# Modulation parts made by VectorE inside the feed-forward stages, with VectorE also making the weights' low halves there

## The reference

```python
def adaln_chunks(cond, w_mod, b_mod):
    m = jax.nn.silu(cond) @ w_mod + b_mod
    return jnp.split(m[:, None, :], N_MOD, axis=-1)          # N_MOD = 9, D = 1024

def pre(h, g, shift, scale):
    return rms_norm(h, g) * (1 + scale) + shift

def swiglu(h, w1, w3, w2):
    return (jax.nn.silu(h @ w1) * (h @ w3)) @ w2             # D_FF = 2816

mx = adaln_chunks(c, w_mod[i], b_mod[i])                      # tokens
mc = adaln_chunks(c_ctx[None], w_mod[i], b_mod[i])            # context
h_x = h_x + 0.5 * mx[2] * ffn1(pre(h_x, g_norm[i, 0], mx[0], mx[1]))
...                                                           # mixer with mx[3..5], ffn2 with mx[6..8]
```

## Time and profile before

| | us |
|---|---|
| median of three runs | 2426.44 (2426.08 to 2431.41) |
| the profiled execution | 2429.39 |
| its span in the trace | 2427.6 |
| PE busy | 2303.7 (95%) |
| DVE busy | 952.8 (39%) |
| ACT busy | 785.6 (32%) |
| POOL busy | 1027.7 (42%) |

### The profile page before, as it was taken

One profiled execution on the slowest core, in us unless ns is written; L12 is line 12 of the kernel. 1 busy time (PEld: TensorE's weight loads), 2 busy tenths in 40 slices (PEclk: granted clock), 3 DMA queues, 4 the chain that ended last, 5 costly groups with the idle time before them and its releaser, 6 DMA issues.

```text
span 2427.6 us, 36791 instructions
## 1 busy us (share of the span) xinstructions
PE 2303.7 (95%) x14268; PEld 1829.4 (75%) x14268; DVE 952.8 (39%) x1611; ACT 785.6 (32%) x1239; POOL 1027.7 (42%) x473
## 2 busy tenths in 40 slices
PE   6998789999879999999999999999999999898999
PEld 2688766767658888887887888887888887547999
DVE  4468646765551131135364121124122114755212
ACT  2443423333323212213223222223222222434443
POOL 0446512323424444443443444443444443304888
PEclk8999879999989999999999999999999999989999
DMA  7334425544543433233432433232433332203655
GB/s 248 91 101 130 148 96 190 178 157 171 216 153 130 130 96 91 90 95 102 150 96 87 165 96 92 91 96 80 164 96 96 96 95 71 76 0 94 184 181 182
DMA packets 82681, 297.37 MB, mean 122 GB/s; under 512 B 9072, under 2 KB 11504, under 8 KB 82288
## 3 DMA queue, kind: packets, MB, share of 16 engines
q1 hardware_dynamic: 82400, 295.03, 37.7%
q10 hardware_dynamic: 144, 0.34, 0.0%
HBM read 294.28 MB, written 1.05 MB: 122 GB/s over the span
## 4 chain that ended last, share of the span: by engine, by line
issue 52%; PE 22%; POOL 19%; DVE 5%; ACT 1%; POOLq 1%; DVEq 0%; ACTq 0%
POOL w_lo L520 19%; PE bank L544 4%; PE bank L548 4%; PE bank L545 4%; PE bank L588 2%; PE bank L1296 1%; PE bank L1307 1%; DVE box L1075 1%; PE bank L919 1%; PE bank L1261 1%; PE bank L1279 0%; PE bank L1252 0%; DVE boxr L1105 0%; DVE boxr L1075 0%; DVE gdn_outer L1646 0%
## 5 line engine op out<-in xcount | busy, mean ns | idle before, releaser
L520 POOL TENSOR_TENSOR w_lo<-w_raw,w_hi 128x1024 fp32r<-128x1024 f32 x383 | 935.4, 2447 | 1175.0 <-ACT w_hi L772 1174.7
L544 PE MATMUL bank<-n_hi,w_lo 128*128 128x512 f32 (+1 forms) x2216 | 799.5, 361 | 31.7 <-POOL w_lo L520 19.5
L548 PE MATMUL bank<-n_lo,w_hi 128*128 128x512 f32 (+1 forms) x2216 | 790.0, 357 | 0.6 <-DVE n_lo L696 0.3
L545 PE MATMUL bank<-n_hi,w_hi 128*128 128x512 f32 (+1 forms) x2216 | 787.3, 355 | 0.0
L772 ACT CAST w_hi<-w_raw 128x1024 fp32r<-128x1024 f32 x383 | 401.2, 1049 | 775.1 <-PE bank L548 768.3
L544 PEld LDWEIGHTS bank<-n_hi,w_lo 128*128 128x128 f32 x2216 | 423.1, 191 | 114.0 <-issue 43.1
L548 PEld LDWEIGHTS bank<-n_lo,w_hi 128*128 128x128 f32 x2216 | 422.7, 191 | 69.0 <-DVE n_lo L696 2.4
L545 PEld LDWEIGHTS bank<-n_hi,w_hi 128*128 128x128 f32 x2216 | 424.8, 192 | 62.6
L2018 DVE TENSOR_TENSOR prod<-silu,bank 128x512 f32<-128x512 f32 (+1 forms) x88 | 54.6, 621 | 727.4 <-PE bank L548 720.1
L544 PE MATMUL bank<-g_hi,w_lo 128*128 128x512 f32 (+1 forms) x768 | 285.2, 371 | 1.1 <-DVE g_lo L2009 1.1
L548 PE MATMUL bank<-g_lo,w_hi 128*128 128x512 f32 (+1 forms) x768 | 283.4, 369 | 0.0
(11 more groups left out here) (315 smaller groups left out, 2017.9 us busy)
## 6 DMA issues: line engine op xcount, KB each, us to landing
w_raw<-in_stream SPq DMA_DIRECT2D x383, 512.0 KB, 3.6
mod_raw<-in_modstream SPq DMA_DIRECT2D x64, 512.0 KB, 5.4
late<-in_modstream SPq DMA_DIRECT2D x56, 512.0 KB, 4.6
w_raw<-in_modstream SPq DMA_DIRECT2D x48, 512.0 KB, 5.2
h<-in_tokens SPq DMA_DIRECT2D x1, 2048.0 KB, 10.2
consts<-in_consts SPq DMA_DIRECT2D x1, 1152.0 KB, 10.0
h<-in_ctx SPq DMA_DIRECT2D x1, 1024.0 KB, 7.5
out<-h SPq DMA_DIRECT2D x8, 128.0 KB, 3.4
```

Source lines behind the costliest of these rows:

```text
L520: nc.gpsimd.tensor_tensor(w_lo[:, slot, :], w_raw[:, slot, :], w_hi[:, slot, :].bitcast(F32), ALU.subtract).then_inc(w_lo_ready, 1)
L544: nc.tensor.matmul(out_ap, wl, hi, start=start, stop=False)
L545: nc.tensor.matmul(out_ap, wh, hi, start=False, stop=False)
L548: return nc.tensor.matmul(out_ap, wh, lo, start=False, stop=stop)
```

## The change

Of the 168 parts 16 stay at the start and 32 in the recurrence (4 a round, at "first" and "last"; three buffers, so that `w_raw` is free and three chunks of the out stage are loaded when the first three of those parts are). PE makes none in the out stage and in the norms. The 120 parts of groups 3 to 10 go to DVE, in ffn0, ffn1 and ffn2: for a part, DVE multiplies 128x1024 weights by one number a partition and adds them to a running sum, once for tokens and once for context (`dve_late`), so 240 instructions in all. They stand at up and down groups that `late_plan` lists, one or two parts at each. When a group is complete, PE sums the running sums over the partitions with eight matmuls of 32x512 (`late_sum`; four for the last group), in the middle of the feed-forward products, and copy, transposes and bias follow there too. In ffn0, ffn1 and ffn2 DVE makes the low halves of the weights as well (`dve_low_half`, 198 chunks of 128x1024) and POOL none; elsewhere POOL makes them as before. The loops over the two halves of these three stages are written out. The late parts have five buffers in place of nine, and their loads are spread over the feed-forward stages in SP's queue. Gains 2 and up and gates 1 and up move from the out stage and the norms to the feed-forward stages.

```diff
-MOD_ROUND = 12
-RECUR_RING, LATE_RING = 6, 9
+MOD_ROUND = 4
+RECUR_RING, LATE_RING = 3, 5
 MOD_EARLY = MOD_PARTS
 MOD_LATE = MOD_EARLY + 8 * MOD_ROUND
-MOD_END = MOD_PARTS * (MOD_GROUPS - 1) + MOD_PARTS // 2
-
-
-LATE_OUT = {10: 4, 11: 4, 12: 4, 13: 4, 14: 3, 15: 2}
-OUT_TURN = 15
-LATE_TURNS = {("sc", 0): (3, 3, 3, None), ("ffn", 1): (2, 0, 7, 8), ("ffn", 2): (5, 4, 0, 9), ("mla", 0): (4, 4, 0, 10)}
+LATE_GROUP0 = MOD_LATE // MOD_PARTS
...
+    ups = [("up", h, f) for h in range(2) for f in range(HALF)]
+    downs = [("down", h, d) for h in range(2) for d in range(KT)]
+    first = [slot for slot in ups[0:8] for _ in range(2)]
+    second = [ups[10]] * 2 + downs[0:8] + [slot for slot in ups[HALF:HALF + 3] for _ in range(2)]
+    third = [slot for slot in ups[HALF + 5:2 * HALF] for _ in range(2)] + [downs[8]] * 2 + [downs[9]] * 2
+    short = [ups[10]] * 2 + downs[0:6]
+    slots, g = {}, LATE_GROUP0
+    for n, plan in ((0, (first, second, third)), (1, (first, second, third)), (2, (first, short))):
+        for places in plan:
+            for q, slot in enumerate(places):
+                slots.setdefault((n,) + slot, []).append((g, q // KT, q % KT))
+            g += 1
...
+for n_ in range(3):
+    g_ = LATE_GROUP0 + 3 * n_
+    LATE_SUM[n_, 0, 19], LATE_COPY[n_, 0, 20], LATE_TURN[n_, 0, 23], LATE_BIAS[n_, 0, 24] = (g_,) * 4
+    if n_ < 2:
+        LATE_SUM[n_, 1, 9], LATE_COPY[n_, 1, 10], LATE_TURN[n_, 1, 13], LATE_BIAS[n_, 1, 15] = (g_ + 1,) * 4
+        LATE_SUM[n_, 1, 26], LATE_COPY[n_, 1, 27], LATE_TURN[n_, 1, 28], LATE_BIAS[n_, 1, 27] = (g_ + 2,) * 4
+    else:
+        LATE_SUM[n_, 1, 5], LATE_COPY[n_, 1, 6], LATE_TURN[n_, 1, 9], LATE_BIAS[n_, 1, 11] = (g_ + 1,) * 4
+LATE_ENDS = [LATE_LAST[LATE_GROUP0 + 2], LATE_LAST[LATE_GROUP0 + 5], LATE_LAST[LATE_GROUP0 + 7]]
+LATE_USES = {0: ((2, 3), (1, 2)), 1: ((4, 5), (3, 4)), 2: ((6,), (5,))}
...
+        g, half, k = LATE_ORDER[q]
         if q >= LATE_RING:
-            sp.wait_ge(mod_used, MOD_LATE + q - LATE_RING + 1)
-        load_mod(sp, MOD_LATE + q)
+            sp.wait_ge(late_used, q - LATE_RING + 1)
+        sp.dma_start(late[:, q % LATE_RING, :], modstream[g * MOD_PARTS + 2 * k + half]).then_inc(late_full[q % LATE_RING], 16)
...
-            if r == 3:
-                sp.wait_ge(w_lo_ready, IN_LOADS)
             if r >= RECUR_RING:
                 sp.wait_ge(mod_used, MOD_EARLY + r - RECUR_RING + 1)
             load_mod(sp, MOD_EARLY + r)
-
-
-        sp.wait_ge(mod_used, MOD_LATE)
-        for i in range(IN_LOADS, IN_LOADS + RING):
-            load_chunk(sp, i, i % RING)
+            if r == 2:
+                for i in range(IN_LOADS, IN_LOADS + RING):
+                    sp.wait_ge(w_lo_ready, i - RING + 1)
+                    load_chunk(sp, i, i % RING)
         sp.wait_ge(d_o, 8)
...
+    def dve_low_half(dve, i):
+        dve.wait_ge(w_hi_ready, i + 1)
+        nc.vector.tensor_tensor(w_lo[:, i % RING, :], w_raw[:, i % RING, :], w_hi[:, i % RING, :].bitcast(F32),
+                                ALU.subtract).then_inc(w_lo_ready, 1)
...
-        low_halves(pool, before_recur, N_STREAM)
-        for i in range(N_STREAM - N_STREAM % RING, N_STREAM):
-            low_half(pool, i, i % RING)
+        low_halves(pool, before_recur, CH_FFN[0] + RING)
+        low_halves(pool, CH_SC + RING, CH_FFN[1] + RING)
+        low_halves(pool, CH_MLA + RING, N_STREAM)
...
+    def late_sum(pe, g):
+
+        pe.wait_ge(late_used, LATE_LAST[g])
+        pe.wait_ge(mod_copied, g)
+        for j in range(4 if g < MOD_GROUPS - 1 else 2):
+            for c in range(2):
+                last = nc.tensor.matmul(bank[MOD_BANK][32 * j:32 * j + 32, :], col(Cols.SEL + 7 - c, 32),
+                                        late_acc[:, c, j, :], start=(c == 0), stop=(c == 1))
+        last.then_inc(late_summed, 1)
+
+    late_next = [0]
+
+    def dve_late(dve, *slot):
+        for g, half, k in LATE_SLOTS.get(slot, ()):
+            q = late_next[0]
             late_next[0] += 1
+            dve.wait_ge(late_full[q % LATE_RING], 16 * (q // LATE_RING + 1))
+            if q:
+                dve.wait_ge(late_used, q)
+            if half == k == 0 and g > LATE_GROUP0:
+                dve.wait_ge(late_summed, g - LATE_GROUP0)
+            part = late[:, q % LATE_RING, :]
+            for c in range(2):
+                acc = late_acc[:, c, 2 * half:2 * half + 2, :].rearrange("p a b -> p (a b)")
+                if k == 0:
+                    last = nc.vector.tensor_scalar(acc, part, cond[:, 1, k, c:c + 1], None, ALU.mult)
+                else:
+                    last = nc.vector.scalar_tensor_tensor(acc, part, cond[:, 1, k, c:c + 1], acc, ALU.mult, ALU.add)
+            last.then_inc(late_used, 1)
...
-    MOD_SLOTS = {"first": 2, "half": 3, "last": 3, "key": 4}
+    MOD_SLOTS = {"first": 2, "last": 2}
...
-            if k == 10:
-                pe.wait_ge(o_n, 3)
-            late_parts(pe, LATE_OUT.get(k, 0))
-            if k == OUT_TURN:
-                pe.wait_ge(o_n, 4)
-                mod_turn(pe, RECUR_LAST + 1)
...
-        for i in range(1, 5):
-            step(dve_gain(dve, i))
-        for i in range(3):
-            step(dve_gate(dve, i))
+        step(dve_gain(dve, 1))
...
+            def late(g, k):
+                if n == 3 or k:
+                    return
+                if (n, half, g) in LATE_SUM:
+                    late_sum(pe, LATE_SUM[n, half, g])
+                if (n, half, g) in LATE_TURN:
+                    mod_turn(pe, LATE_TURN[n, half, g])
...
+            def low_halves_to(j):
+                if n < 3:
+                    while chunk[0] <= j:
+                        dve_low_half(dve, CH_FFN[n] + half * HALF_CHUNKS + chunk[0] + RING)
+                        chunk[0] += 1
+
+            if n < 3 and half == 0:
+                dve.wait_ge(w_lo_ready, CH_FFN[n] + RING)
             for f in range(HALF):
+                low_halves_to(max(2 * f, FFN_FIRST - 2))
                 g = g0 + 2 * f + 1
                 dve.wait_ge(gate_ready, half * HALF + (hid0 + f + 1))
                 dve.wait_ge(linear_done, half * MARKS + GROUP_DONE[key][2 * f + 1])
@@ -2019,17 +2084,24 @@
                                         ALU.mult).then_inc(groups_read, 2)
                 if f:
                     low(f - 1)
+                late(half, 2 * f + 1, "up", f)
             low(HALF - 1)
             for d in range(KT):
+                low_halves_to(2 * HALF + (HALF * d + HALF - 1) // TILES_PER_CHUNK)
                 dve_residual(dve, key, 2 * HALF, gate, w, d, half * MARKS, half * HALF_GROUPS, squares)
+                late(half, 2 * HALF + d, "down", d)
```

191 lines of the change are left out of this document (94 added, 97 removed).

## The result

The changed kernel is slower: 2448.33 us (median of five runs, 2443.5 to 2453.54) against 2431.17 for the kernel before in the same comparison (2426.08 to 2432.83), ratio 1.0076 with a 95% interval of 1.0056 to 1.0097. The forecast was 2425 with a range from 2411 to 2442. Of the 23 us between forecast and result 5 lie in the kernel before itself: it had a median of 2426.44 when the forecast was made and 2431.17 here. The ratio does not have them: by it the change costs 0.76%, some 18 us. The profiled execution took 2448.78, its span 2447.0.

What follows compares the result with a forecast made beforehand. PE, busy 95%, was taken to bound the kernel, taking turns with DVE in the recurrence. A -17, B -13, D +5.5, E +18.8, F +4 summed to -1.7, taking the median from 2426.4 to 2425 us, range 2411 to 2442.

Steps and rivals of the forecast that it cites:

- A: Recurrence, 64 parts gone: 17 us gained (8 to 24) of 37 removed, the rest hidden beside or lost to DVE.
- rival 1: Recurrence and out stage: all PE time comes back, 30 and 19 us gained, 2406 us; under 2419 given 0.30.
- B: Out stage, 21 parts gone: 13 us gained (5 to 20), limited by DVE's context squares stretched beside a busy POOL.
- C: End of the recurrence, eighth "key" slot and last turn: no gain, since DVE's and POOL's last outputs are waited for.
- D: Four norms without parts: 5.5 us lost (1 to 10), gaps -2.0, slow-clock starts behind them +7.5.
- E: Sums and turns within feed-forward products: 18.8 us lost (14 to 28): sums 14, turns 4, waits 0.8.
- third rival: Feed-forward sums run in strict order, 4.6 us each in place of 1.85: 21 us slower, 2446 us; chance 0.07.
- F: DVE's new load in ffn0, ffn1, ffn2: 4 us lost (0 to 15), mostly low halves late at half starts.
- fourth rival: DVE's running sums at half speed, a part at 4.7 us: 93 us slower, 2518 us; chance 0.02.
- Rival 2: Feed-forward stages and exits: low halves late behind running sums on DVE; 2436 us, or 2445 with A low; chance 0.18.

Runs made afterwards that it cites:

- e4: Changed kernel, but GpSimd makes all low halves again while DVE keeps the 120 parts: 2459.52 us, ratio 1.0131 to the kernel before.

## Why the prediction was wrong, point by point

- **A, the recurrence, is the step that failed** (-17, measured +5.8). The hidden shares were well read: PE's waits grew by 15.9 us at just the places named. What the sum left out is that a PE which idles there is granted the lower clock for part of the time: 104 us of the gap at half speed in place of 36. The prediction counted that loss behind idle norms, where the earlier trace rows showed 0.56, and took the recurrence's 1.00 for granted, although that 1.00 had been measured with the very parts in place that the change removed. Nor did any rival have it: rival 1 had only more gain. With the clock nearly held by filler the removal of "key" alone gained 3.6 where I had counted 8, of "half" and "last" with "key" kept 2 us were lost where I had counted 12.
- **B, the out stage**: -13, measured -13.7, and by the mechanism named: DVE's squares beside a busy POOL. A line of the changed kernel shows one at 2.6 us, and PE waits for the residual behind them. The stretch was sized wrong (14 squares and 12 sums cost 23.8 us before and 29.1 after, 5 more, not 24), but they stood where all of it held PE. That the number agrees so well is in part luck:

```profile
668.75 2.60 DVE L794 TENSOR_TENSOR nt<-h 128x256 f32<-128x256 f32 x1
...
677.36 0.58 PE L574 MATMUL bank<-n_hi,w_lo 128*128 128x256 f32 x1 [7.08 <-DVE h L1909]
```

- **C**: the wait that ends the recurrence grew from 5.5 to 7.9 us, so what was taken away there bought nothing, as forecast; it lies in the table's row on the recurrence.
- **D, the norms**: the order's 2.3 us were right, but the gaps came out at 10.8, 8.5, 10.8 and 11.6 in place of 9.9, 7.6, 9.9 and 9.9: the norm's own matmuls ran cold, 0.9 each and 1.7 ahead of mla. The slow starts were forecast at 7.5; the first 61 products of the changed kernel against those before give 1.6 (sc), 2.5 (ffn1), 2.2 (ffn2) and 0.6 (mla): 6.9.
- **E**: eight sums at 1.97, not 7.5 at 1.85: 15.7 instead of 14. The last one was counted as half and took as long as the others, as three parts take as long as four: its four matmuls are two, one behind the other, in each of two column groups, and the other two groups stand empty. Turns 0.35 or, at two places, 0.87: 3.9. The third rival, sums in strict order at 4.6, is refuted by L639's 1.94. The Trainium skill (TensorE: Matmul & The Clock Gate, What overlaps and what doesn't) has matmuls start and end in strict order. As the third rival reads that rule the trace doesn't agree, for matmuls in different column groups.
- **F**: prices exact (1.280, 1.224 us; forecast 1.28, 1.22). The fourth rival, half speed of the running sums, is refuted by L660's 1280 ns for 1024 columns. The Trainium skill (Vector Engine (DVE) Microarchitecture Reference, Points that are easy to get wrong) states half throughput for this instruction with two fp32 sources in SBUF; this trace doesn't agree. Lateness: 0.8 at each of two half starts, less than the 4 forecast. E and F together are the growth of ffn0, ffn1 and ffn2 without the cold starts, 8.0 + 9.4 + 4.9 = 22 us, forecast 22.8; the terms named here come to 21. The number is that near since two misses cancel, the sums 1.7 higher and the lateness 2.4 lower.
- **Rival 2** (2436, DVE's order) had the right sign. Its part on the exits was right, 3 us each as it said (3.3 on the mean), though 0.9 and more of that is the clock and not the order; its part on the half starts was not, since PE waited 0.7 at two of them, not 2 to 3 at each. Its other condition, ACT's casts behind late low halves, did not arise.

In one line: the traces differ by 19.4 us where -1.7 was forecast. Of these 21 us, A is 23 and D's gaps 4.5; unchanged code gave back 4, and B, the slow starts, E and F together 2.

## What to carry to other kernels

Work that looks like a load on TensorE may be what keeps its clock up. Before such work is moved away, the clock must be read not at the place where the work goes, but at the place that it leaves, and a 1.00 there is no promise once it is gone: price each removed slot with useless work in its place, and read the clock with the time: here the recurrence got 9 us shorter by idle matmuls, and the clock was what had changed. The gain of a removal is then only what the other engine leaves, times a clock that may fall; and an engine's exit work (a residual that a norm waits for) should stand ahead of anything that has slack, since a late exit also lets the clock fall under the norm's own matmuls.

## What was not expected of the hardware

- 64 parts' worth of idle matmuls made the recurrence 9 us shorter (328.5 to 319.4), and those at "half" and "last" alone 12.6 us (to 315.9).
- Four fp32 matmuls of 32x512 in two column groups took PE 1.94 us, as long as eight in four (1.97).
- A wait of 3.4 and 4.3 us of PE in a full stage (e4) was followed by some microseconds of products at 0.43 us each in place of 0.23.
- The same DVE instruction of 128x1024 took 1.275 to 1.289 us with GpSimd idle, and up to 3.449 in e4, where GpSimd works beside it, with the median still 1.284: a median by line hides it.
- ffn3, whose code no kernel changed, took between 185 and 194 us in one execution or another. Why was not looked into.
